# Where the buffers of a two-block transformer kernel lie: 1,920 bytes of small tensors first, the large ones at multiples of 2,048

## The reference

```python
# first block
x = x + 0.5 * swiglu(rms_norm(x, ffn1_norm), ...)            # d_ff = 2816
u = rms_norm(x, mix_norm) @ w_in                             # latent attention (8 heads) and block attention (8 heads)
x = x + concat(mla_attention(...), moba_attention(...)) @ w_out
x = x + 0.5 * swiglu(rms_norm(x, ffn2_norm), ...)
x = rms_norm(x, final_norm)
# second block, two layers: i = 0 mixes with ssd_mixer, i = 1 with retention
for i in range(2):
    h = h + mixer_i(rms_norm(h, mix_norm[i]))
    h = h + peer_ffn(rms_norm(h, ffn_norm[i]), ...)
    g = sigmoid(rms_norm(h, ple_norm[i]) @ ple_gate[i])
    h = h + g * (p[i] @ ple_proj[i])
```

```python
hid = gelu(einsum('tkd,td->tk', u[idx], x))       # 128 picked rows of u for each token
out = einsum('tk,tkd->td', gate * hid, v[idx])    # and the same rows of v
```

## Time and profile before

| | |
|---|---|
| median of three runs | 2378.12 us (2377.91 to 2379.96) |
| span of the profiled execution, first to last instruction | 2377.4 us |
| mean granted clock of TensorE in it | 0.987 of full speed |
| busy: PE, DVE, ACT, POOL | 88%, 73%, 33%, 28% |
| bytes moved by the DMA queues | 726.83 MB, mean 306 GB/s |
| of them on POOL's queue (the gathers and two loads of `wide`) | 539.00 MB, 54.8% of 16 engines' span |

### The profile page before, as it was taken

How to read it: one execution, slowest core, us unless ns; L and a number is a source line. 1 busy time by engine, 2 the same in 40 slices (tenths; PEclk the granted TensorE clock), 3 DMA queues, 4 the chain that set the end, 5 groups by cost and what they waited for, 6 DMA issues and landing times. The chain is left out here.

```text
span 2377.4 us, 26604 instructions
## 1 busy us (share of the span) xinstructions
PE 2099.5 (88%) x9124; PEld 1360.9 (57%) x9124; DVE 1741.8 (73%) x3737; ACT 788.0 (33%) x1479; POOL 654.0 (28%) x520
## 2 busy tenths in 40 slices
PE   8999999999999888887877778999898987777777
PEld 7998889999877544432322226988554532222224
DVE  6545665558766888878887876656888887878786
ACT  4334653346584221211211116345322121211114
POOL 0000000000100455444544440000455554444440
PEclk9999999999989999999999999999999999999999
DMA  6554425554425999999999995545999999999994
GB/s 253 193 176 172 147 89 183 189 178 158 142 89 204 410 419 420 419 420 421 420 420 421 420 379 207 212 142 195 364 419 420 420 420 420 420 420 420 420 418 170
DMA packets 101355, 726.83 MB, mean 306 GB/s; under 512 B 11633, under 2 KB 11889, under 8 KB 13425
## 3 DMA queue, kind: packets, MB, share of 16 engines
q0 software_dynamic: 74016, 539.00, 54.8%
q1 hardware_dynamic: 25200, 181.41, 21.0%
q10 hardware_dynamic: 2016, 4.89, 0.6%
HBM read 724.21 MB, written 1.05 MB: 305 GB/s over the span
## 5 line engine op out<-in xcount | busy, mean ns | idle before, releaser
L2090 PE MATMUL bank<-arena 128*128 128x512 f32 (+4 forms) x2104 | 919.6, 567 | 187.1 <-DVE arena L1969 183.9
L742 POOL DMA_INDIRECT arena<-in_uv,expert x434 | 545.3, 1257 | 885.0 <-PE bank L2090 486.7
L2090 PEld LDWEIGHTS bank<-arena 128*128 128x128 f32 (+2 forms) x2104 | 358.2, 194 | 663.9 <-DVE arena L1969 425.5
L2019 DVE SCALAR_TENSOR_TENSOR arena<-arena,xn 128x1024 f32<-128x1024 f32 x434 | 530.5, 1222 | 81.0 <-DMA arena<-in_uv,expert 78.5
L1337 DVE TENSOR_TENSOR lw_rounded<-lw,w_hi 128x2048 fp32r<-128x2048 f32 x153 | 352.8, 2307 | 205.1 <-ACT w_hi L795 202.0
L1233 ACT ACTIVATE act_h<-hid 128x1 f32<-128x1 f32 x512 | 103.8, 203 | 1047.1 <-DVE arena L2019 888.2
L2090 PE MATMUL bank<-xT_hi,w_hi 128*128 128x256 f32 x1320 | 413.2, 313 | 8.7 <-DVE xT_lo L1382 5.2
L795 ACT ACTIVATE w_hi<-lw 128x2048 fp32r<-128x2048 f32 (+1 forms) x173 | 312.9, 1817 | 242.2 <-PE bank L2090 219.0
L2090 PE MATMUL bank<-xT_lo,w_hi 128*128 128x256 f32 x1320 | 373.6, 283 | 0.0
L2090 PE MATMUL bank<-xT_hi,lw_rounded 128*128 128x256 f32 x1256 | 355.8, 283 | 0.0
L1969 DVE TENSOR_SCALAR arena<-consts,act_h,weight 128x128 f32<-128x128 f32 x512 | 193.9, 379 | 123.8 <-ACT act_h L1233 115.9
(11 more groups left out here) (270 smaller groups left out, 1959.3 us busy)
## 6 DMA issues: line engine op xcount, KB each, us to landing
lw<-in_units SPq DMA_DIRECT2D x165, 1024.0 KB, 4.8
arena<-in_uv,expert POOLq DMA_INDIRECT x434
arena<-in_units SPq DMA_DIRECT2D x4, 1024.0 KB, 7.8
wide<-in_wide POOLq DMA_DIRECT2D x2, 1024.0 KB, 8.9
gain<-in_gains ACTq DMA_DIRECT2D x4, 512.0 KB, 9.6
wide<-in_units SPq DMA_DIRECT2D x2, 1024.0 KB, 6.9
h<-in_x SPq DMA_DIRECT2D x2, 512.0 KB, 4.2
arena<-in_ret_consts ACTq DMA_DIRECT2D x1, 1024.0 KB, 4.7
```

The lines of the kernel that those rows point to most:

```text
L742: nc.gpsimd.indirect_dma_start(out=row_slot(slot), out_offset=None, in_=table, in_offset=bass.IndirectOffsetOnAxis(ap=expert[par][:, k:k + ...
L2019: V.scalar_tensor_tensor(row_slot(slot)[:, 0:D], row_slot(slot)[:, 0:D], 1.0, xn[:, tile, :], ALU.mult, ALU.mult, accum_out=hid[par][:, k: ...
L2090: return nc.tensor.matmul(o, lhsT, rhs, start=start, stop=stop, **more)
```

## The change

The instructions of all five engines, their order, their waits and their sizes stay as they are. What is changed is the order in which the tensors are allocated, and by that their addresses. Twenty-three small tensors (`conv` to `sel_p`), which take 1,920 bytes with the padding between them, are allocated first. Behind them the address is 18,432, a multiple of 2,048, and the large ones follow, each a multiple of 2,048 bytes long but for `arena`, which has its odd length and is followed by `consts`, `gain_col`, `warm` and `vecs`. From `sel_ab` on, the last fifteen small tensors keep their addresses, and so does the descriptor area of POOL's DMAs (bytes 0 to 16,383).

| tensor | bytes | address before | mod 2,048 / 256 / 64 | address after | mod 2,048 / 256 / 64 |
|---|---|---|---|---|---|
| h | 8,192 | 16,512 | 128 / 128 / 0 | 18,432 | 0 / 0 / 0 |
| xn | 8,192 | 24,704 | 128 / 128 / 0 | 26,624 | 0 / 0 / 0 |
| xT_hi, xT_lo | 8,192 each | 32,896, 41,088 | 128 / 128 / 0 | 34,816, 43,008 | 0 / 0 / 0 |
| lw | 32,768 | 49,280 | 128 / 128 / 0 | 51,200 | 0 / 0 / 0 |
| w_hi | 24,576 | 82,048 | 128 / 128 / 0 | 83,968 | 0 / 0 / 0 |
| gain | 8,192 | 106,624 | 128 / 128 / 0 | 108,544 | 0 / 0 / 0 |
| wide | 8,192 | 115,168 | 480 / 224 / 32 | 116,736 | 0 / 0 / 0 |
| arena | 95,232 | 131,808 | 736 / 224 / 32 | 124,928 | 0 / 0 / 0 |
| consts | 4,752 | 123,360 | 480 / 224 / 32 | 220,160 | 1,024 / 0 / 0 |
| vecs | 2,944 | 128,128 | 1,152 / 128 / 0 | 225,280 | 0 / 0 / 0 |

All addresses are multiples of 32 before and after. The slots of the gathers and of `lw` are 8,192 bytes long, so each begins at the same remainder as its tensor.

```diff
-        h = sb("h", [P, NT, D])
-        xn = sb("xn", [P, NT, D])
-        xT = (sb("xT_hi", [P, KD, S], F32R),
-              sb("xT_lo", [P, KD, S], F32R))
-        lw, w_lo = twins("lw", [P, RING, UNIT])
-        w_hi = sb("w_hi", [P, HIGHS, UNIT], F32R)
-        gain = sb("gain", [P, 2, D])
-        gain_col = sb("gain_col", [P, len(T_OF), KD])
-        warm = sb("warm", [P, N_FINAL + 3])
-        wide = sb("wide", [P, DI])
-        consts = sb("consts", [P, C_END])
-        vecs = sb("vecs", [P, V_END])
         conv = sb("conv", [P, CONV_DIM // P, 5])
         posf = sb("posf", [P, NT])
...
         grs = sb("grs", [P, NT, 4])
+        cos = sb("cos", [P, NT, HALF])
+        sin = sb("sin", [P, NT, HALF])
...
+        sel_p = sb("sel_p", [P, TOPK], U32)
+
+        h = sb("h", [P, NT, D])
+        xn = sb("xn", [P, NT, D])
+        xT = (sb("xT_hi", [P, KD, S], F32R),
+              sb("xT_lo", [P, KD, S], F32R))
+        lw, w_lo = twins("lw", [P, RING, UNIT])
+        w_hi = sb("w_hi", [P, HIGHS, UNIT], F32R)
+        gain = sb("gain", [P, 2, D])
+        wide = sb("wide", [P, DI])
+        arena, arena_rounded = twins("arena", [P, ARENA])
+        consts = sb("consts", [P, C_END])
+        gain_col = sb("gain_col", [P, len(T_OF), KD])
+        warm = sb("warm", [P, N_FINAL + 3])
+        vecs = sb("vecs", [P, V_END])
...
-        ARENA = 23808
-        arena, arena_rounded = twins("arena", [P, ARENA])
```

More of the change, by code:

```diff
@@ L130 @@
 SECOND_FROM = 2
+ARENA = 23808
 C_ID, C_EPS, C_FIRST = 0, 128, 132
@@ L300, in build @@
         grs = sb("grs", [P, NT, 4])
+        cos = sb("cos", [P, NT, HALF])
+        sin = sb("sin", [P, NT, HALF])
+        lss = sb("lss", [P, 2, NT])
+        lms = sb("lms", [P, 2, NT])
+        lrt = sb("lrt", [P, 2, NT])
+        lrs = sb("lrs", [P, 2, NT])
+        nmax = sb("nmax", [P, SOFT_RING, 2])
+        psum_of = sb("psum_of", [P, NT, 2 * HEADS])
+        rsum = sb("rsum", [P, NT, 2 * HEADS])
+        top_v = sb("top_v", [P, 2, TOPK])
+        top_i = sb("top_i", [P, 2, TOPK], U32)
+        top_f = sb("top_f", [P, 2, TOPK])
+        sel_s = sb("sel_s", [P, TOPK])
+        sel_p = sb("sel_p", [P, TOPK], U32)
[12 more added lines that the diff above has]
+        vecs = sb("vecs", [P, V_END])
         ident = consts[:, C_ID:C_ID + P]
@@ L370, in build @@
         probT = region(at, "probT", SOFT_RING, TRI)
[L373 to L381, removed]
         at = [0]
@@ L461, in build @@
         pt_whole = vecs[:, 0:2 * S].rearrange("p (k s) -> p k s", s=S)
[L462 to L466, removed]
         sel_ab = sb("sel_ab", [P, 2, TOPK], U32)
```

## The result

The changed kernel takes 2349.54 us (median of four runs, 2348.5 to 2351.77) against 2378.01 us; the ratio is 0.9884 with an interval of 0.9873 to 0.9896. It is 28.5 us or 1.2% faster. I forecast 2369 us, in a range that ended at 2355.

What follows compares the result with a forecast made beforehand. The prediction took gather transfers to bound the two peer_ffn stages and compute the rest. Span 2377.4 less 9.3 us for gathers, engines and units zero, gave 2368.1, plus 0.7 about 2369 us; eight-in-ten range 2355 to 2381.

Steps and rivals of the forecast that it cites:

- What bounds the kernel: Both peer_ffn stages are bound by gather transfers, some eight standing in line; the other stages by compute.
- the ends: End of each peer_ffn stage: SP waits for a late row, so gather savings reach the end one for one.
- The gathers' price: peer_ffn gathers: 466 into arena and wide gain 0.02 us each, 46 into gain nothing; 9.3 us in all.
- the cleaner pair: Landings in peer_ffn: gain, at 0 modulo 64, against arena slots, at 32; a gather into gain 0.02 us shorter.
- upper end: Back-to-back unit loads into lw against gathers into the arena: 41 ns apart, the most the address could cost.
- the bound that I gave: Upper bound of the gathers' gain: all 512 at lw's pitch, 21 us, 2357 us.
- Lone loads: Unit loads alone on the queues, into lw or wide, don't see the address; zero gain for units.
- the larger rival: Gathers: every start off 256 bytes costs, gain's too, growing with distance; 23 us, 2355, or 34 us, 2344; chance 0.08.
- The engines: DVE dot products and PE matmuls: address gains zero; 3.9 us possible on 512-column matmuls, 4 us kept for the range.
- The 0.7 us: Median time lies 0.7 us above the profiled execution's span, added to the forecast span of 2368.1 us.
- No change: Gathers: gain's difference comes from something else, or the reading side sets the pitch; 2378 us, chance 0.18.
- slower: Large buffers sharing one remainder of 2,048 collide; 0.02 us on all 512 gathers, 10 us, 2388 us; chance 0.12.

Runs made afterwards that it cites:

- e5: Changed kernel with all large buffers, arena included, shifted to start at 128 modulo 2,048; 2367.6 us.
- e11: Kernel before with each indirect gather replaced by a direct load of 128 neighbouring rows on the same queue; 2375.51 us.
- e12: Changed kernel with each indirect gather replaced by a direct load of 128 neighbouring rows on the same queue; 2346.33 us, two executions only.
- e8: Changed kernel with all large buffers shifted to start at 32 modulo 2,048; 2373.3 us.
- e1: Changed kernel with the large buffers back at 128 modulo 2,048, all but arena and wide; 2353.74 us, ratio 0.9906.
- e2: Changed kernel with the arena alone of the large buffers shifted to 224 modulo 2,048; 2373.09 us, ratio 0.9987.
- e9: Changed kernel with the arena alone at 64 modulo 2,048, the other large buffers at 0; 2368.61 us, ratio 0.9963.
- e4: Changed kernel with all large buffers shifted to start at 64 modulo 2,048; 2369.2 us.
- e7: Changed kernel with all large buffers shifted to start at 96 modulo 2,048; 2368.3 us.
- e3: Changed kernel with h to gain at 256 and wide and arena at 768 modulo 2,048; 2349.7 us, ratio 0.9886.

## Why the prediction was wrong

**What bounds the kernel: right.** The two stages were the gathers' and the ends were tied to them. The pitch fell by 41 ns, and the line of gathers stayed: on the chain a gather now takes 19.35 to 19.50 us from issue to landing, 20.12 before. One reading of the page was loose: PE's row falls to 7 or 8 in nine of the second stage's eleven slices, and two stand at 9.

**The gathers' price: the failed step.** "Afterwards all slots are at 0 modulo 64", priced at 0.02 us for 466 gathers by what `gain` showed, and at nothing for the 46 into `gain`. The price is 41 ns, and `gain` pays too, because 256 is the bound and not 64. I took `gain` for an aligned slot. At 128 it was itself a dear one: e5, with all at 128, runs at 2.486 us, only 8 ns under the 2.494 of 224. So the contrast I weighed as the cleaner pair was between two dear starts. By their packets it was smaller than I read it: in the kernel before, the median from a gather into `gain` to the next is 2.488 us. The 0.02 us were mostly scatter of the landings. In the kernel after, where every slot is at 0, triples with `wide` in the middle still come out at 4.87 us (7 of them) against 4.90 with the arena. That I came near half the true 41 ns was chance.

The pair that I set aside as an upper end, `lw` at 427 against the gathers at 420 GB/s, 41 ns, had the right size, though not for the reason that one would give: `lw` too lay at 128. e11 and e12 show that scattered rows, one of the two things that I put in the way, cost nothing. Why `lw` ran at the full rate from 128 is shown in part. In e8, with `lw` at 32, two of its loads still follow each other 2.453 us apart. A short burst pays nothing on the gathers' queue either: in the kernel before, the first five gathers of a layer have a median row of 309 ns, and from the seventh on it is 313. So a few loads in a row don't show the price; whether many on `lw`'s queue would, no run shows.

The size: 18.0 us between the first and last gathers of the layers against my 9.3. All 512 at 41 ns would be 21 us, the bound that I gave.

**Lone loads: right and misleading.** They don't see the address; the median row of a unit takes 309 ns in `lw` and in `wide`, before and after. I used it against the larger rival, though it says nothing of a long line of loads.

**The engines: the other half of the miss.** DVE's zero was right, 1222 and 1223 ns. On the 409 ns against 403 I wrote "if that were the address and not the company they keep, 656 x 6 ns = 3.9 us would come back" and took zero: it was the address, and with it changed the group's mean is 403. I had taken the term at zero on no more than a doubt, and the 4 us that I meant to keep for the range are not in it: its end, 2355, is the larger rival's price alone. e8 gives the term 4.8 us by itself. What I could not read from before was that it hangs on both operands, as e1, e2 and e9 show; `xT_hi` and `w_hi` shared their remainder in that kernel, arena and weights did not. This and the gathers make 23 of 28.5 us. The rest, some 5 us, lies outside the gathers and seems to go with the same pair. In the profiled executions the time outside the two gather stages is 1082.3 us before and 1079.9 in e11, which has its addresses; 1075.8 to 1078.0 in e1, e2 and e9; and 1070.1 to 1077.1 in the nine runs in which all large buffers share one remainder of 256. That is more than e8's median gives, and two profiles of one layout differ by up to 2.4 us, so the split of these 5 us stays open. The 0.7 us that I put between span and time is 2.1 to 2.2 in the profiled executions of all experiments; it drops out of the difference.

**The rivals.** Mine that a start off 256 costs, `gain`'s too, was right in kind; it had 0.08. I made its price grow with the distance, which e4 to e7 refute, and so got 23 us from the wrong sum. The Trainium skill's rule ("DMA: Bandwidth & Descriptors", "How a descriptor splits into AXI transactions"), that transactions start at multiples of 256 bytes, agrees with 256 as the bound (e3, e4 to e8), for writes into the working memory as well. An estimate by its beats, six more against two, would make 192 cost three times what 64 does; measured, both cost 32 ns. No change and slower had 0.30 between them; e3 shows the common remainder harmless.

## What to carry to other kernels

Where a stage is bound by a long line of DMA loads, start each destination row at a multiple of 256 bytes: here, with rows of 8 KiB, it takes 1.6% off the time between loads, and padding for it costs nothing where small tensors can stand in front. Check it in the long line, since lone loads, short bursts and one off-256 buffer among aligned ones show no price. If a reference case is to stand for "aligned", make sure that it is: a contrast of two dear cases looks like a small effect. A term that is set to zero on a doubt has to be added into the range, not only mentioned: here it was worth some 5 us. And a matmul's few ns can hang on how its two operands lie to each other, so a layout should be tried as a whole.

## What was not expected of the hardware

- Rows of 8 KiB written from a start off 256: 4 ns each in the long line of gathers at 64, 96, 128 and 192, and 5 ns at 32 and 224; nothing in a lone load, in two loads in a row, in the first five gathers of a layer, or where one gather in ten starts at 128 and the others at 0.
- A matmul of 512 columns takes 389 ns when its two operands start at the same remainder of 256 (0, 32, 64, 96, 128, 192) and 392 to 398 ns at distances of 128, 224, 96 and 64.
- Matmuls of 256 columns go the other way: 283 to 284 ns at the same remainder, 280 and 281 with the moving operand 64 and 224 above the stationary one's. Why is open.
